# Memory keys and values as three rounded products instead of one fp32 product, and one tile's output products issued before a wait

## The chip, the cores and the metric

One core of a Trainium2 chip runs the whole kernel. The metric is device time in microseconds of one execution; the median of 3 runs of the kernel before is 2779.76 us (2779.39 to 2781.21).

## The reference, cut to what matters

Two transformer-like blocks follow each other on 1024 tokens of width 1024, all in fp32. The change lies in the first: after its mixing and attention the sum goes through an output projection, and a cross-attention to 256 memory tokens comes next.

```python
x = x + jnp.concatenate([y_f, y_a], axis=-1) @ w_out[l]
x = x + memory_cross_attention(rms_norm(x, g_mem_q[l]), rms_norm(mem, g_mem_kv[l]),
                               w_mem_q[l], w_mem_kv[l], w_mem_o[l])
...
def memory_cross_attention(hq, mn, w_mem_q, w_mem_kv, w_mem_o):
    q = (hq @ w_mem_q).reshape(B, S, MEM_HEADS, MEM_HEAD_DIM)
    k, v = jnp.split(mn @ w_mem_kv, 2, axis=-1)      # mn: 256 x 1024, w_mem_kv: 1024 x 2048
    s = jnp.einsum("bshd,bmhd->bhsm", q, k).astype(jnp.float32) * (MEM_HEAD_DIM ** -0.5)
    p = jax.nn.softmax(s, axis=-1).astype(v.dtype)
    o = jnp.einsum("bhsm,bmhd->bshd", p, v).reshape(B, S, D)
    return o @ w_mem_o
```

A mixture of experts and the second block follow; the change does not touch them.

## The kernel before, in words

The program is written out engine by engine, each engine's instructions in a fixed order with semaphores between them. PSUM has eight banks; a helper (`Bank`, line 87 on) gives each product a bank in turn, `begin` makes TensorE wait until the bank's last use is read, `end` signals that it is full, `wait` lets a reader wait for that, `done` and `read` tell and await that it has been read out.

Most products are made in three passes: an operand is rounded to fp32r (`hi`), the rest is kept as a second fp32r part (`lo`), and the product is hi*hi + hi*lo + lo*hi, each an fp32r matmul. ScalarE makes `hi` with a copy, VectorE (or GpSimd) makes `lo` with a subtraction, often in the place of the raw data. The memory keys and values are an exception: they are plain fp32 products. The stages around the change, in order:

- **End of the first attention.** Heads' outputs are gathered in four chunks of 128 features (`mixa`). Chunks 0 to 2 are rounded and split early; chunk 3 comes from the very last heads: ScalarE copies (line 1440), VectorE adds and multiplies (2075, 2076), ScalarE rounds the chunk (1404) and VectorE makes its remainder (2078, signal `block1_lo`).
- **Output products `y1`** (loop at 2797). For each of 8 token tiles and both halves j of the columns, `mixed(t, j, k)` (2750) gives three matmuls of 512 columns for chunk k. Tile 0's products with chunks 0 to 2 are issued already inside the attention's loop, behind the transposes of the last two score tiles; the wait for `block1_lo` comes next, then chunk 3 of tile 0, then tiles 1 to 7 whole. VectorE adds each result to X (`mixed_in`, 2079; addition at 2084). Before tile 7 TensorE transposes the normalised memory tokens (`nm`), and VectorE multiplies the gain in (`gained`, 1889) into `mnT`.
- **Key loop** (2813). For c in 0 to 7: one block `mk`, eight fp32 products of a 128x128 weight tile with the 256 memory tokens (line 2820), then the two groups of transposes of token tile c (`n2`, line 2591), after a wait for the normalised tile. ScalarE's loop (1458): squares of tile c (1287), the rounded copies of the tokens of tile c-1 (1456), then the copy of key block c out of PSUM (1279). GpSimd makes the reciprocal root (1018, 1019). VectorE's loop: scaling of tile t (1885), then the two remainders of its tokens (2101).
- **Value loop** (2825). Eight blocks `mv` through the helper `product` (2605). ScalarE rounds each (1478), VectorE makes its remainder (2118). After blocks 0 to 3 ScalarE and VectorE split the first half of the query weights (`mem_round`, line 1473, and `mem_rest`, line 2111), after block 7 the second half.
- **Query products `mq`** (2831). Three passes, 512 columns, 24 matmuls a block.

Weights come over SyncE's queue into a ring of three 2 MB slots (`fetch`, issues at 909). The memory weights are four pieces `mkv0` to `mkv3`: `mkv0` is fetched at the attention's end, `mkv1` and `mkv2` are issued when the last `y1` product is done, `mkv3` after key block 3, the query weights `mq0` after key block 7 and `mq1` after value block 3.

Of the kernel before, what the change touches and what calls it, by code (L numbers as in the profile page):

```python
# [137 lines left out]
def build(nc, A, out):  # L138
    sems = {}
    ctx = ExitStack()  # L140
    with ctx:
# [490 lines left out]
        memx = mem(GB0, 2048).rearrange("p (m d) -> p m d", m=2)  # L632
        mnT = mem(SPARE, 2048).rearrange("p (k s) -> p k s", k=KC)
        KM = mem(GB0 + 4096, 2048).rearrange("p (k s) -> p k s", k=KC)
        VT_hi, VT_lo = (mem_r(at_, 2048).rearrange("p (c s) -> p c s", c=8) for at_ in (GB0 + 6144, HN_AT))
# [640 lines left out]
        def _(act):  # L1276
# [173 lines left out]
            for m in range(2):  # L1450
                act.wait_ge(sem(f"mem_in{m}"), 16)
                square(memx[:, m, :], D, st[:, 48 + m:49 + m], HN[m]).then_inc(sem("norm_ssq"), 1)
            def token_hi(t):
                for j in range(2):
                    b = bk.wait(act, ("n2", t, j))
                    nc.scalar.activation(xm_hi[t // 4][:, 4 * j:4 * j + 4, tile(t % 4)], b4(b), ACT.Copy).then_inc(sem("psum_hi"), 1)

            for c in range(8):
                bk.read(act, ("y1", c, 1))
                bk.wait(act, ("n2", c - 2, 1) if c >= 2 else ("nm", c, 1))  # L1460
                square(X[:, c, :], D, st[:, 52 + c:53 + c], HN[c % 2]).then_inc(sem("norm_ssq"), 1)
                if c >= 1:
                    token_hi(c - 1)
                b = bk.wait(act, ("mk", c))
                copy(("mk", c), KM[:, c, :], PS[:, b, 0:MEM])
# [8 lines left out]

            for n in range(2):
                for c in range(4 * n, 4 * n + 4):
                    b = bk.wait(act, ("mv", c))
                    nc.scalar.activation(VT_hi[:, c, :], PS[:, b, 0:MEM], ACT.Copy).then_inc(sem("psum_hi"), 1)
                mem_round(f"mq{n}", R_MQ)
            for c, h in MQ:  # L1480
# [387 lines left out]
        def _(dve):  # L1868
# [210 lines left out]
            def mixed_in(t):  # L2079
                dve.wait_ge(sem(f"x_tile{t}"), 64)  # L2080
                for j in range(2):
                    b = bk.wait(dve, ("y1", t, j))
                    x = X[:, t, NB * j:NB * j + NB]
                    bk.done(v.tensor_tensor(x, x, PS[:, b, :], ALU.add), ("y1", t, j))

            for t in range(T - 1):
                mixed_in(t)
                if t >= T - 3:
                    m = t - (T - 3)
                    scaled("nm", m, memx[:, m, :], HN[m], st[:, 50 + m:51 + m])  # L2090
            for j in range(2):
                for m in range(2):
                    gained(("nm", m, j), mnT[:, 4 * j:4 * j + 4, tile(m)], R_MKV, 4 * j)
            mixed_in(T - 1)
            for t in range(T):
                scaled("n2", t, X[:, t, :], HN[t % 2], st[:, 60 + t:61 + t])
                for j in range(2):
                    dve.wait_ge(sem("psum_hi"), XM_HI + 2 * t + j + 1)
                    b = bk.at[("n2", t, j)][0]
                    hi, lo = (x[t // 4][:, 4 * j:4 * j + 4, tile(t % 4)] for x in (xm_hi, xm_lo))  # L2100
                    bk.done(v.tensor_tensor(lo, b4(b), value(hi), ALU.subtract), ("n2", t, j))

            def mem_rest(name, n, row=None, ks=range(KC)):
                for k in ks:
                    c = slice(NB * k, NB * k + NB)
                    dve.wait_ge(sem("part_hi"), n + k + 1)
                    lo, raw, hi = mem_lo[name][:, c], mem_raw[name][:, c], value(mem_hi[name][:, c])
# [5 lines left out]

            for n in range(2):
                for c in range(4 * n, 4 * n + 4):
                    dve.wait_ge(sem("psum_hi"), VT_HI + c + 1)
                    b = bk.at[("mv", c)][0]
                    bk.done(v.tensor_tensor(VT_lo[:, c, :], PS[:, b, 0:MEM], value(VT_hi[:, c, :]), ALU.subtract), ("mv", c))
                mem_rest(f"mq{n}", UP_N + KC * n, R_MQ)
            mem_rest("mo0", UP_N + 2 * KC)  # L2120
            for kind, t in att2_steps():
# [10 lines left out]
                elif kind == "vw":  # L2132
                    for h in range(4):
# [5 lines left out]
                        if t == 0 and h >= 2:  # L2139
                            mem_rest("mo1", UP_N + 3 * KC, None, range(4 * (h - 2), 4 * (h - 2) + 4))  # L2140
                elif kind == "pt":
# [445 lines left out]
        def _(pe):  # L2587
# [209 lines left out]
            for t in range(T):  # L2797
                if t == T - 1:
                    for m in range(2):
                        pe.wait_ge(sem("norm_hn"), HNORM["nm"] + m + 1)  # L2800
                        for j in range(2):
                            turns(("nm", m, j), HN[m][:, NB * j:NB * j + NB])
                for j in range(2):
                    if t >= 1:
                        bk.begin(pe, ("y1", t, j))
                        for k in range(3):
                            mixed(t, j, k)
                if t == 0:
                    pe.wait_ge(sem("block1_lo"), 8)
                for j in range(2):  # L2810
                    bk.end(mixed(t, j, 3), ("y1", t, j))

            for c in range(8):
                if c % 4 == 0:
                    w_wait(pe, f"mkv{c // 4}")
                b = bk.begin(pe, ("mk", c))
                for k in range(KC):
                    if c == 0 and k % 4 == 0:
                        bk.read(pe, ("nm", 0, k // 4)), bk.read(pe, ("nm", 1, k // 4))
                    ins = mm(PS[:, b, 0:MEM], wview(f"mkv{c // 4}")[:, k, tile(c % 4)], mnT[:, k, :], start=(k == 0), stop=(k == KC - 1))  # L2820
                bk.end(ins, ("mk", c))
                pe.wait_ge(sem("norm_hn"), HNORM["n2"] + c + 1)
                for j in range(2):
                    turns(("n2", c, j), HN[c % 2][:, NB * j:NB * j + NB])
            for c in range(8):
                if c % 4 == 0:
                    w_wait(pe, f"mkv{2 + c // 4}")
                product(("mv", c), lambda k: wview(f"mkv{2 + c // 4}")[:, k, tile(c % 4)], lambda k: mnT[:, k, :], KC, lambda b: PS[:, b, 0:MEM])
            for t in range(T):
                bk.read(pe, ("n2", t, 0)), bk.read(pe, ("n2", t, 1))  # L2830
            for c, h in MQ:
                w1, w2 = (x[f"mq{c // 4}"].rearrange("p (k n) -> p k n", k=KC) for x in (mem_hi, mem_lo))
                b = bk.begin(pe, ("mq", c, h))
                for k in range(KC):
                    if c % 4 == 0 and h == 0:
                        pe.wait_ge(sem("part_lo"), UP_N + KC * (c // 4) + k + 1)
                    x1, x2 = xm_hi[h][:, k, :], xm_lo[h][:, k, :]
                    mm(PS[:, b, :], w1[:, k, tile(c % 4)], x1, start=(k == 0), stop=False)
                    mm(PS[:, b, :], w1[:, k, tile(c % 4)], x2, start=False, stop=False)
                    ins = mm(PS[:, b, :], w2[:, k, tile(c % 4)], x1, start=False, stop=(k == KC - 1))  # L2840
                bk.end(ins, ("mq", c, h))
            for c in range(8):
                bk.read(pe, ("mk", c)), bk.read(pe, ("mq", c, 0))
            for kind, t in att2_steps():
# [11 lines left out]
                elif kind == "vw":  # L2856
# [4 lines left out]
                    for h in range(4):  # L2861
                        for d in range(2):
                            pe.wait_ge(sem("part_lo"), UP_N + KC * (2 + t) + 2 * h + d + 1)
                        for m in range(2):
# [349 lines left out]
```

## Time and profile before

| what | value |
|---|---|
| median of 3 runs | 2779.76 us |
| profiled execution | 2780.26 us |
| its span | 2778.3 us |
| TensorE matmul busy | 2726.2 us (98%) |
| weight loads busy | 2281.4 us (82%) |
| VectorE, ScalarE, GpSimd busy | 1800.1, 1259.2, 439.2 us |
| mean granted TensorE clock | 0.996 of 2.4 GHz |

Every row gives a start in microseconds from the start of the span and a duration. A matmul's record lasts longer than the distance to the next, since matmuls are pipelined: the distance of starts is the pace. Records of weight loads are shown as an operation of their own (PEld). Operands are named by the region of memory (`w_f` is the fp32 view of the ring, `w_f32r` its fp32r view, `ps` is PSUM). The bracket at the end of a row is the idle time of the engine before it and what ended it. The granted clock is a share of 2.4 GHz; 0.50 is 1.2 GHz.

### The profile page before, as it was taken

The page shows a single profiled execution, that of the slowest core. Times are in us where ns is not written, and L with a number is a line of the kernel's source. Part 1 is how long each engine was busy: PE and PEld are TensorE (multiplying, and loading weights), DVE is VectorE, ACT ScalarE, POOL GpSimd, SP SyncE. Part 2 cuts the span into 40 slices and gives each one's busy share as a digit, 9 for nine tenths or more (in the row PEclk, how much of TensorE's full clock was granted, in tenths as well). Part 3 has the DMA queues.
Part 4 walks back from the last instruction along what each step waited for, and adds up shares of the span by engine and source line. Part 5 has one row for each costly group of instructions (what it writes and reads, how often), then busy time and mean ns, then how long its engine had stood idle before and what let it go on. Part 6 is the DMA issues. An engine that isn't in the chain of part 4 may idle for free.

```text
span 2778.3 us, 36356 instructions
## 1 busy us (share of the span) xinstructions
PE 2726.2 (98%) x14436; PEld 2281.4 (82%) x14436; DVE 1800.1 (65%) x2497; ACT 1259.2 (45%) x2026; POOL 439.2 (16%) x393
## 2 busy tenths in 40 slices
PE   8999999999999999999999999999999999999998
PEld 7978888788884888888888887878888868888898
DVE  3646888330546888888885968988886572110575
ACT  4333787141432777777776124454454453111101
POOL 1500231000011211111102000000001043221341
PEclk9999999999999999999999999999999999999999
DMA  4041000420217999999982121030121221110141
GB/s 140 31 154 46 31 1 1 165 93 32 92 67 294 391 396 396 396 396 396 395 326 69 61 104 49 20 118 28 60 72 42 94 76 46 46 46 31 60 145 61
DMA packets 141604, 379.79 MB, mean 137 GB/s; under 512 B 11952, under 2 KB 45234, under 8 KB 141309
## 3 DMA queue, kind: packets, MB, share of 16 engines
q1 hardware_dynamic: 126140, 325.22, 30.9%
q0 software_dynamic: 12560, 42.74, 4.9%
q10 hardware_dynamic: 2736, 9.50, 0.9%
q8 instruction: 116, 1.90, 0.3%
q14 instruction: 52, 0.42, 0.0%
HBM read 341.13 MB, written 35.26 MB: 135 GB/s over the span
## 4 chain that ended last, share of the span: by engine, by line
PE 91%; DVE 4%; ACT 2%; DMA 1%; issue 1%; POOL 0%; SPq 0%; ACTq 0%; POOLq 0%; DVEq 0%
PE ps L2988 8%; PE ps L2989 8%; PE ps L2990 8%; PE ps L2591 7%; PE ps L2973 6%; PE ps L2975 6%; PE ps L2974 6%; PE ps L3082 3%; PE ps L3084 3%; PE ps L3083 3%; PE ps L2605 3%; PE ps L3129 2%; PE ps L3094 1%; PE ps L3096 1%; PE ps L3095 1%; PE ps L3114 1%
## 5 line engine op out<-in xcount | busy, mean ns | idle before, releaser
L2310 DVE SCALAR_TENSOR_TENSOR b_f<-b_f,small_f 128x1023 f32<-128x1023 f32 (+14 forms) x240 | 304.3, 1268 | 27.0 <-ACT small_f L1279 13.8
L2988 PE MATMUL ps<-x_f32r,w_f32r 128*128 128x512 f32 x480 | 187.9, 392 | 4.3 <-DVE b_f L2507 3.6
L2990 PE MATMUL ps<-x_f32r,w_f32r 128*128 128x512 f32 x480 | 187.4, 390 | 0.0
L2974 PE MATMUL ps<-w_f32r,a_f32r 128*128 128x512 f32 x456 | 177.4, 389 | 0.0
L2989 PE MATMUL ps<-ht_f32r,w_f32r 128*128 128x512 f32 x416 | 162.5, 391 | 0.0
L3083 PE MATMUL ps<-w_f32r,a_f32r 128*128 128x512 f32 x384 | 149.9, 390 | 0.0
L2974 PE MATMUL ps<-x_f32r,a_f32r 128*128 128x512 f32 x312 | 121.4, 389 | 0.0
L1279 ACT ACTIVATE x_f<-ps 128x512 f32<-128x512 f32 (+1 forms) x184 | 91.0, 533 | 44.4 <-PE ps L2591 21.0
L1209 POOL TENSOR_TENSOR w_f32r<-w_f,w_f32r 128x2048 fp32r<-128x2048 f32 x23 | 110.2, 4793 | 1.9
L2988 PEld LDWEIGHTS ps<-x_f32r,w_f32r 128*128 128x128 f32 x480 | 90.4, 188 | 23.7 <-issue 4.9
L2990 PEld LDWEIGHTS ps<-x_f32r,w_f32r 128*128 128x128 f32 x480 | 90.5, 189 | 18.9
L2200 DVE TENSOR_TENSOR w_f32r<-w_f,c_f32r 128x2048 fp32r<-128x2048 f32 x38 | 86.1, 2285 | 26.3 <-ACT c_f32r L1540 26.3
L2973 PE MATMUL ps<-c_f32r,a_f32r 128*128 128x512 f32 x256 | 101.0, 394 | 0.3 <-issue 0.3
L2973 PE MATMUL ps<-ht_f32r,a_f32r 128*128 128x512 f32 x256 | 101.2, 395 | 0.0
L2973 PE MATMUL ps<-b_f32r,a_f32r 128*128 128x512 f32 x256 | 99.7, 389 | 0.3 <-issue 0.3
L2975 PE MATMUL ps<-ht_f32r,a_f32r 128*128 128x512 f32 x256 | 99.9, 390 | 0.0
L2974 PEld LDWEIGHTS ps<-w_f32r,a_f32r 128*128 128x128 f32 x456 | 85.7, 188 | 17.2
L2975 PE MATMUL ps<-b_f32r,a_f32r 128*128 128x512 f32 x256 | 99.7, 389 | 0.0
L2975 PE MATMUL ps<-c_f32r,a_f32r 128*128 128x512 f32 x256 | 99.7, 389 | 0.0
L2988 PE MATMUL ps<-ht_f32r,w_f32r 128*128 128x512 f32 x256 | 99.6, 389 | 0.0
L2990 PE MATMUL ps<-ht_f32r,w_f32r 128*128 128x512 f32 x256 | 99.6, 389 | 0.0
L2057 DVE TENSOR_REDUCE small_f<-ps 128x1 f32<-128x1024 f32 x64 | 78.1, 1220 | 30.8 <-PE ps L2770 30.3
(578 smaller groups left out, 7870.6 us busy)
## 6 DMA issues: line engine op xcount, KB each, us to landing
w_f<-in_w_exp_up SPq DMA_DIRECT2D x40, 1024.0 KB, 10.3
w_f<-in_w_exp_down SPq DMA_DIRECT2D x38, 1024.0 KB, 10.2
w_f<-in_w_exp_gate SPq DMA_DIRECT2D x36, 1024.0 KB, 8.8
x_f<-in_w_exp_gate SPq DMA_DIRECT2D x28, 1024.0 KB, 8.6
x_f<-in_w_exp_down SPq DMA_DIRECT2D x26, 1024.0 KB, 11.0
x_f<-in_w_exp_up SPq DMA_DIRECT2D x24, 1024.0 KB, 10.3
w_f<-in_w_in SPq DMA_DIRECT2D x22, 1024.0 KB, 5.1
w_f<-in_w_in SPq DMA_DIRECT2D x10, 2048.0 KB, 8.1
```

The lines of the kernel that those rows point to most:

```text
L1209: nc.gpsimd.tensor_tensor(mem_r(slot, k * n), mem(slot, k * n), value(mem_r(slot + 2048, k * n)), ALU.subtract).then_inc(sem("split"), 1)
L1279: ins = nc.scalar.activation(dst, src, ACT.Copy, scale=scale)
L2200: v.tensor_tensor(unit_lo(n), unit_raw(n), value(unit_hi(n)), ALU.subtract).then_inc(sem("unit_lo"), 1)
L2310: ins = v.scalar_tensor_tensor(C_conv[k][:, d:S], U_conv[k][:, 0:S - d], cols[:, k, R_TAP + j:R_TAP + j + 1], C_conv[k][:, d:S], ALU.mult, ...
L2591: return nc.tensor.transpose(dst, src, ident[0:n, 0:n])
L2973: mm(o, x1, w1[:, k, c], start=(kk == 0), stop=False)
L2974: mm(o, x1, w2[:, k, c], start=False, stop=False)
L2975: ins = mm(o, x2, w1[:, k, c], start=False, stop=(kk == KC - 1))
L2988: mm(o, l1, r1, start=(k == 0), stop=False)
L2989: mm(o, l1, r2, start=False, stop=False)
L2990: ins = mm(o, l2, r1, start=False, stop=(k == n - 1))
L3083: mm(PS[:, b, :], x1[:, k, :], lo[:, k, :], start=False, stop=False)
```

## The change

`y1`: TensorE issues tile 1's products with chunks 0 to 2 right before the wait for chunk 3, and tile 1 later adds only its chunk 3.

Keys and values: each of the 16 blocks becomes 24 fp32r matmuls of 256 columns (`mem_columns`). For block p ScalarE rounds a column chunk of 128 of its 2 MB weight piece (8 x 128 elements on each partition) into one of six buffers (`mkv_round`), and VectorE puts the remainder in the place of the raw weights (`mkv_rest`). The memory tokens are split too, in two halves. ScalarE and VectorE run two blocks ahead of TensorE; blocks 2 to 5 wait for the last `y1` product, since their buffers lie where the output weights were. The rounding of the first query weight piece moves: chunks 4 to 7 after value block 5, chunks 0 to 3 (their home holds the rounded tokens) after block 7, and TensorE takes the chunks in that order.

```diff
+        mn_lo, mn_hi = (mem_r(at_, 2048).rearrange("p (k s) -> p k s", k=KC) for at_ in (SPARE, GC0))
+        MKV_N = 18
+        MQ_ORDER = {"mq0": [4, 5, 6, 7, 0, 1, 2, 3]}
+        mkv_home = [GC0 + 2048, GC0 + 3072] + [GA0 + 1024 * i for i in range(4)]
+        def mkv_parts(p):
+            at_, c = W0 + 4096 * wslot(seq[f"mkv{p // 4}"]), tile(p % 4)
+            raw, lo = (x.rearrange("p (k n) -> p k n", k=KC)[:, :, c] for x in (mem(at_, 4096), mem_r(at_, 4096)))
+            return raw, mem_r(mkv_home[p % 6], 1024).rearrange("p (k n) -> p k n", k=KC), lo
...
+            def mkv_round(p):
+                w_wait(act, f"mkv{p // 4}")
+                if 2 <= p < 6:
+                    bk.wait(act, ("y1", T - 1, 1))
+                elif p >= 6:
+                    bk.wait(act, ("mk", p - 6) if p < 14 else ("mv", p - 14))
+                raw, hi, lo = mkv_parts(p)
+                nc.scalar.activation(hi, raw, ACT.Copy).then_inc(sem("part_hi"), 1)
+            mkv_round(0)
+            mkv_round(1)
+            for j in range(2):
+                bk.read(act, ("nm", 0, j)), bk.read(act, ("nm", 1, j))
+                nc.scalar.activation(mn_hi[:, 4 * j:4 * j + 4, :], mnT[:, 4 * j:4 * j + 4, :], ACT.Copy).then_inc(sem("part_hi"), 1)
...
                 if c >= 1:
                     token_hi(c - 1)
+                mkv_round(c + 2)
                 b = bk.wait(act, ("mk", c))
...
-            for n in range(2):
-                for c in range(4 * n, 4 * n + 4):
-                    b = bk.wait(act, ("mv", c))
-                    nc.scalar.activation(VT_hi[:, c, :], PS[:, b, 0:MEM], ACT.Copy).then_inc(sem("psum_hi"), 1)
-                mem_round(f"mq{n}", R_MQ)
+            for c in range(8):
+                if c < 6:
+                    mkv_round(c + 10)
+                b = bk.wait(act, ("mv", c))
+                nc.scalar.activation(VT_hi[:, c, :], PS[:, b, 0:MEM], ACT.Copy).then_inc(sem("psum_hi"), 1)
+                if c == 5:
+                    mem_round("mq0", R_MQ, range(4, 8))
+            mem_round("mq0", R_MQ, range(0, 4))
+            mem_round("mq1", R_MQ)
...
+            def mkv_rest(p):
+                dve.wait_ge(sem("part_hi"), UP_N + (p + 1 if p < 2 else p + 3))
+                raw, hi, lo = mkv_parts(p)
+                v.tensor_tensor(lo, raw, value(hi), ALU.subtract).then_inc(sem("part_lo"), 1)
             for t in range(T - 1):
                 mixed_in(t)
+                if 3 <= t < 5:
+                    mkv_rest(t - 3)
...
+            for j in range(2):
+                dve.wait_ge(sem("part_hi"), UP_N + 3 + j)
+                c = slice(4 * j, 4 * j + 4)
+                v.tensor_tensor(mn_lo[:, c, :], mnT[:, c, :], value(mn_hi[:, c, :]), ALU.subtract).then_inc(sem("part_lo"), 1)
             mixed_in(T - 1)
             for t in range(T):
                 scaled("n2", t, X[:, t, :], HN[t % 2], st[:, 60 + t:61 + t])
+                mkv_rest(t + 2)
...
+            for c in range(8):
+                if c < 6:
+                    mkv_rest(c + 10)
+                dve.wait_ge(sem("psum_hi"), VT_HI + c + 1)
+                b = bk.at[("mv", c)][0]
+                bk.done(v.tensor_tensor(VT_lo[:, c, :], PS[:, b, 0:MEM], value(VT_hi[:, c, :]), ALU.subtract), ("mv", c))
+                if c == 5:
+                    mem_rest("mq0", UP_N + MKV_N, R_MQ, range(4, 8))
+            mem_rest("mq0", UP_N + MKV_N, R_MQ, range(0, 4))
+            mem_rest("mq1", UP_N + MKV_N + KC, R_MQ)
...
-                for j in range(2):
-                    if t >= 1:
-                        bk.begin(pe, ("y1", t, j))
+                for u in ([1] if t == 0 else [t] if t >= 2 else []):
+                    for j in range(2):
+                        bk.begin(pe, ("y1", u, j))
                         for k in range(3):
-                            mixed(t, j, k)
+                            mixed(u, j, k)
                 if t == 0:
                     pe.wait_ge(sem("block1_lo"), 8)
...
+            def mem_columns(name, p):
+                raw, w1, w2 = mkv_parts(p)
+                b = bk.begin(pe, name)
+                o = PS[:, b, 0:MEM]
+                if p >= 2:
+                    pe.wait_ge(sem("part_lo"), UP_N + p + 3)
+                for k in range(KC):
+                    if p == 0 and k % 4 == 0:
+                        pe.wait_ge(sem("part_lo"), UP_N + 3 + k // 4)
+                    mm(o, w1[:, k, :], mn_hi[:, k, :], start=(k == 0), stop=False)
+                    mm(o, w1[:, k, :], mn_lo[:, k, :], start=False, stop=False)
+                    ins = mm(o, w2[:, k, :], mn_hi[:, k, :], start=False, stop=(k == KC - 1))
+                bk.end(ins, name)
...
```

## Rows read from the trace of the kernel before

**Rows 1.** The page: the head, then the engines of the chain that ended last.

```profile
span 2778.3 us, 36356 instructions
...
PE 91%; DVE 4%; ACT 2%; DMA 1%; issue 1%; POOL 0%; SPq 0%; ACTq 0%; POOLq 0%; DVEq 0%
```

**Rows 2.** Groups by line, each shape apart, 484 to 700 us: busy us, mean ns.

```profile
L2820 PE MATMUL ps<-spare_f,w_f 128*128 128x256 f32 x128 | 28.9, 379 | 0.0
L2605 PE MATMUL ps<-spare_f,w_f 128*128 128x256 f32 x128 | 27.8, 379 | 0.0
```

**Rows 3.** TensorE in order of time, 480 to 612 us: start, duration, line, idle before.

```profile
494.54 0.38 PE L2591 MATMUL ps<-small_f 128*128 128x128 f32 x2
498.72 0.79 PE L2753 MATMUL ps<-a_f32r,w_f32r 128*128 128x512 f32 x1 [3.80 <-DVE w_f32r L2078]
...
504.00 0.41 PE L2753 MATMUL ps<-a_f32r,w_f32r 128*128 128x512 f32 x1
...
505.16 0.39 PE L2755 MATMUL ps<-ht_f32r,w_f32r 128*128 128x512 f32 x1
...
511.96 0.39 PE L2755 MATMUL ps<-a_f32r,w_f32r 128*128 128x512 f32 x1
```

**Rows 4.** Stretches: length, busy per engine (TensorE, weight loads, VectorE, ScalarE, GpSimd), clock.

```profile
500.00:504.00 4.00, 4.00 (x10) 3.04 (x10) 1.28 (x2) 0.89 (x1) 0.00 (x0) 0.50 1.02 407
504.00:508.00 4.00, 4.00 (x19) 3.32 (x18) 0.30 (x1) 1.41 (x4) 0.77 (x2) 1.00 1.03 414
```

**Rows 5.** The chain that ended last, 470 to 720 us, in order of time.

```profile
497.44 1.24 DVE w_f32r L2078
```

**Rows 6.** All engines in order of time, 532 to 580 us: one turn of the key loop.

```profile
543.34 3.61 PE L2820 MATMUL ps<-spare_f,w_f 128*128 128x256 f32 x16
...
559.78 1.04 PE L2591 MATMUL ps<-small_f 128*128 128x128 f32 x8
559.98 0.39 ACT L1279 ACTIVATE b_f<-ps 128x256 f32<-128x256 f32 x1 [1.93 <-PE ps L2820]
560.26 1.05 ACT L1287 ACTIVATE small_f<-x_f 128x1024 f32<-128x1024 f32 x1
...
560.65 3.62 PE L2820 MATMUL ps<-spare_f,w_f 128*128 128x256 f32 x16
...
561.30 1.07 ACT L1456 ACTIVATE ht_f32r<-ps 128x512 fp32r<-128x512 f32 x2
...
561.92 1.29 DVE L2101 TENSOR_TENSOR ht_f32r<-ps,ht_f32r 128x512 fp32r<-128x512 f32 x2 [2.38 <-ACT ht_f32r L1456]
563.12 0.74 DVE L1885 TENSOR_SCALAR small_f<-x_f,small_f 128x1024 f32<-128x1024 f32 x1
...
564.11 1.04 PE L2591 MATMUL ps<-small_f 128*128 128x128 f32 x8
```

**Rows 7.** Line 2989, each shape apart: duration ns min/median/max, first and last start.

```profile
L2989 PEld LDWEIGHTS ps<-w_f32r,a_f32r x256: 188/192/192, 2678.6 to 2770.4; 128*128 128x128 f32 x128
L2989 PE MATMUL ps<-w_f32r,a_f32r x256: 283/283/283, 2678.7 to 2770.5; 128*128 128x256 f32 x128
```

**Rows 8.** TensorE in order of time again, where transposes give way to fp32r matmuls.

```profile
485.40 0.47 PE L2753 MATMUL ps<-ht_f32r,w_f32r 128*128 128x512 f32 x1
485.71 0.39 PE L2754 MATMUL ps<-ht_f32r,w_f32r 128*128 128x512 f32 x1
```

**Rows 9.** Lines 1404 and 2078, each shape apart, 380 to 720 us.

```profile
L1404 ACT ACTIVATE w_f32r<-w_f x3: 1053/1056/1057, 392.5 to 496.3; 128x1024 fp32r<-128x1024 f32 x3
...
L2078 DVE TENSOR_TENSOR w_f32r<-w_f,w_f32r x1: 1226/1226/1226, 497.4 to 497.4; 128x1024 fp32r<-128x1024 f32 x1
```

**Rows 10.** DMA issues of 543.3 to 543.8 us: count, KB each, us to landing.

```profile
w_f<-in_w_mem_kv SPq DMA_DIRECT2D x1, 2048.0 KB, 7.8
```

**Rows 11.** Lines 1473 and 2111, each shape apart, 380 to 720 us.

```profile
L1473 ACT ACTIVATE c_f32r<-w_f,small_f x8: 707/708/712, 592.3 to 596.5; 128x512 fp32r<-128x512 f32 x8
...
L2111 DVE SCALAR_TENSOR_TENSOR w_f32r<-w_f,small_f,c_f32r x8: 744/746/753, 593.0 to 597.7; 128x512 fp32r<-128x512 f32 x8
```

More of the change, by code:

```diff
@@ L2105, in mem_rest @@
                     c = slice(NB * k, NB * k + NB)
-                    dve.wait_ge(sem("part_hi"), n + k + 1)
+                    dve.wait_ge(sem("part_hi"), n + MQ_ORDER.get(name, list(range(KC))).index(k) + 1)
                     lo, raw, hi = mem_lo[name][:, c], mem_raw[name][:, c], value(mem_hi[name][:, c])
@@ L2112, in mem_rest @@
                     ins.then_inc(sem("part_lo"), 1)
[L2114 to L2120, printed above, removed]
+            for c in range(8):
[8 more added lines that the diff above has]
+            mem_rest("mq1", UP_N + MKV_N + KC, R_MQ)
+            mem_rest("mo0", UP_N + MKV_N + 2 * KC)
             for kind, t in att2_steps():
@@ L2139, in _ @@
                         if t == 0 and h >= 2:
-                            mem_rest("mo1", UP_N + 3 * KC, None, range(4 * (h - 2), 4 * (h - 2) + 4))
+                            mem_rest("mo1", UP_N + MKV_N + 3 * KC, None, range(4 * (h - 2), 4 * (h - 2) + 4))
                 elif kind == "pt":
@@ L2811, in _ @@
                     bk.end(mixed(t, j, 3), ("y1", t, j))
-            for c in range(8):
[L2814 to L2821, printed above, removed]
+            def mem_columns(name, p):
[11 more added lines that the diff above has]
+                bk.end(ins, name)
+            for c in range(8):
+                mem_columns(("mk", c), c)
                 pe.wait_ge(sem("norm_hn"), HNORM["n2"] + c + 1)
@@ L2825, in _ @@
             for c in range(8):
-                if c % 4 == 0:
-                    w_wait(pe, f"mkv{2 + c // 4}")
-                product(("mv", c), lambda k: wview(f"mkv{2 + c // 4}")[:, k, tile(c % 4)], lambda k: mnT[:, k, :], KC, lambda b: PS[:, b, 0:MEM])
+                mem_columns(("mv", c), 8 + c)
             for t in range(T):
@@ L2833, in _ @@
                 b = bk.begin(pe, ("mq", c, h))
-                for k in range(KC):
+                order = MQ_ORDER.get(f"mq{c // 4}", list(range(KC)))
+                for i, k in enumerate(order):
                     if c % 4 == 0 and h == 0:
-                        pe.wait_ge(sem("part_lo"), UP_N + KC * (c // 4) + k + 1)
+                        pe.wait_ge(sem("part_lo"), UP_N + MKV_N + KC * (c // 4) + i + 1)
                     x1, x2 = xm_hi[h][:, k, :], xm_lo[h][:, k, :]
-                    mm(PS[:, b, :], w1[:, k, tile(c % 4)], x1, start=(k == 0), stop=False)
+                    mm(PS[:, b, :], w1[:, k, tile(c % 4)], x1, start=(i == 0), stop=False)
                     mm(PS[:, b, :], w1[:, k, tile(c % 4)], x2, start=False, stop=False)
-                    ins = mm(PS[:, b, :], w2[:, k, tile(c % 4)], x1, start=False, stop=(k == KC - 1))
+                    ins = mm(PS[:, b, :], w2[:, k, tile(c % 4)], x1, start=False, stop=(i == KC - 1))
                 bk.end(ins, ("mq", c, h))
@@ L2862, in _ @@
                         for d in range(2):
-                            pe.wait_ge(sem("part_lo"), UP_N + KC * (2 + t) + 2 * h + d + 1)
+                            pe.wait_ge(sem("part_lo"), UP_N + MKV_N + KC * (2 + t) + 2 * h + d + 1)
                         for m in range(2):
```

## The prediction

> **What bounds the kernel now.** I read the page first: TensorE is on the chain that ended last for 91% of a span of 2778.3 us [rows 1], so a change pays when it shortens TensorE's own stream or closes a hole in it. The profiled execution took 2780.26 us, 2.0 more than its span and 0.5 more than the median of the runs (2779.76). Sums are differences within the profiled execution, taken off the median at the end.
>
> Next the groups by line, for the two sets of memory products. Each fp32 product is two matmul records, so 128 records are 64 products, and the two groups together keep TensorE busy without a hole [rows 2]. One block of 16 records runs from 560.65 to 564.11: 3.46 us, or 216 ns for a record [rows 6]. Sixteen blocks are 55.4 us.
>
> Then TensorE in order of time, where the first attention ends. It issues its last transposes at 494.54 (0.38 us), and the next matmul starts at 498.72 with 3.80 us of idle before it, released by VectorE's remainder of the last mixed chunk [rows 3, 5]. The twelve matmuls from 498.72 to 504.00 take 5.28 us; thirty at 505.16 to 511.96 take 6.80, so 0.227 each. The granted clock says why: 0.50 from 500 to 504, which is the 1.2 GHz level, and 1.00 right after, the 2.4 GHz level [rows 4]. Before it fell TensorE had stood idle for those 3.80 us.
>
> Last, one turn of the key loop, engine by engine [rows 6]. TensorE never stands there, but this hides a chain nearly as long as its own work, which matters below.
>
> **Part 1, the second tile's products ahead of the wait.** Six groups of three matmuls (two column halves, three chunks) move from behind the wait to ahead of it; they need chunks 0 to 2 alone, and banks 2 and 3, which the last score tile left before its transposes. Nothing is added, no DMA is moved. 18 x 0.227 = 4.1 us of work goes into a hole of 3.80 us, and the hole is gone: 3.8 us won. TensorE then never stops, so the clock should not fall: 5.28 - 12 x 0.227 = 2.6 us more. Two tiles now end close together; VectorE's two additions per tile, of the size of the remainders in [rows 6] (1.29 us), fit easily in the 24 x 0.227 = 5.4 us that TensorE spends on a tile, so that costs nothing. Part 1: **6.4 us**.
>
> **Part 2, three rounded passes.** 128 fp32 products of 432 ns become 384 fp32r matmuls of 256 columns. The trace has that form with three passes: line 2989 and its two neighbours run 256 each from 2678.7 to 2770.5, 91.8 us over 765 gaps, 0.120 us each with a weight load per matmul [rows 7]. A block becomes 24 x 0.120 = 2.88 us, all sixteen 46.1: **9.3 us** won. I take 0.120 as it is the same mix; the bounds are 0.108 (the half of an fp32 record's 216 ns) and 0.192, a load in the open, which is a rival below.
>
> Against it stands a small loss: after transposes the first fp32r matmul keeps 0.31 us to the next instead of 0.23 [rows 8]. Eight switches in the key loop: 0.6 us.
>
> **Part 2's new work.** ScalarE gets a rounding copy of 1024 elements per block, 1.06 us as line 1404, VectorE a subtraction of 1.23 us as line 2078 [rows 9]: sixteen of each, and two of each for the memory tokens. What covers each:
> - *Blocks 0 and 1 and the tokens.* The two blocks fall between the additions, in that same idle. The tokens' parts must be there when the key products start: VectorE has four gain multiplications of about 0.65 and two subtractions of 1.23 to do, 5.1 us, while TensorE has its last transposes and the last tile, 0.87 + 5.4 = 6.3; ScalarE's two copies run beside them. Nothing; without the 1.2 us to spare, at most the second subtraction's 1.2 us.
> - *Key loop, ScalarE.* From the key copy to the end of the token copies it now takes 559.98 to 562.37, 2.4 us [rows 6]; with 1.06 more it is 3.5, against a TensorE turn of 2.88 + 0.08 + 0.87 = 3.83. It fits by 0.4 us. The copy stands before the wait for the next key block, behind everything that the token chain needs of this turn.
> - *Key loop, VectorE.* 1.29 + 0.74 + 1.23 = 3.3 us a turn, also under 3.83, and the subtraction stands behind the scaling that TensorE waits for.
> - *Weights.* ScalarE now needs the second 2 MB piece for block 4 in its third turn, not TensorE in the fifth. It is issued as the y products end and lands 7.8 us later [rows 10]; ScalarE asks for it 2.88 + 3.83 + 2.5 = 9.2 us after the key products start. About 1.2 us to spare. If it were late, the delay would pass into copies and the chain, and cost its own length.
> - *Value loop.* A turn is 2.88 us; ScalarE has 1.06 and a copy of 256 columns (0.39 in [rows 6]), VectorE 1.23 and under 0.65: covered. The six buffers for rounded parts are handed back six blocks earlier.
> - *Query weights.* The low half of their rounded home holds the tokens' rounded part until the last value block. So four pieces come after it, and TensorE begins with the other four: 12 x 0.227 = 2.7 us of cover. The first late piece needs a copy of 0.39, then 0.71 and 0.75 [rows 11], ready at 1.9; VectorE's pace of 0.75 a piece against TensorE's 0.68 eats 0.2 more. Nothing, with 0.6 us to spare; without it the price is about 2 us once.
>
> **What is late next: the token chain.** The end of issue of a key block (559.78) releases the key copy (559.98), the squares (560.26), the two token copies (561.30), VectorE's two remainders (561.92), the next scaling (563.12 to 563.86), and only then the next token's transposes, at 564.11: 4.33 us from block to transposes [rows 6]. TensorE's own turn before is 0.87 + 3.46 = 4.33, so the chain is hidden with nothing to spare. After the change the own turn is 3.83. A wait s at one set of transposes also moves the next block back, so the next wait is 0.50 - s: waits alternate between 0.5 and 0, four in seven turns, **2.0 us** lost. Bounds: 0 (part of the 4.33 was the queue and not the chain) and 8 x 0.5 = 4.0 us (each turn at 4.33).
>
> **Sum.** 6.4 + 9.3 - 0.6 - 2.0 = 13.1 us. Everything behind waits for TensorE's progress (the query products follow at once, the later weights are fetched when blocks end), so the gain is kept to the end: 2779.76 - 13.1 = **2766.7 us**; for the profiled execution 2767.2.
>
> **Rivals.**
> - *TensorE's work alone sets the key loop.* For it: no idle shows today. Against: the scaling ends 0.25 us before the transposes, too close to be free. Gain 15.1: 2764.7 us.
> - *ScalarE or the chain holds every turn at 4.33.* If the strided rounding copy takes over 0.4 us more than line 1404's, ScalarE is the bound. The key loop then wins nothing, the value loop 8 x 0.58: gain 6.4 + 4.6 = 11.0, 2768.8 us. A late second weight piece lands near here too.
> - *The clock falls all the same.* It fell after idle; with no idle nothing in these rows lets it fall. 2.6 us less: 2769.3 us.
> - *The moved products do not start early.* If a bank or operand is held, part 1 is worth nothing: gain 6.7, 2773.1 us, still 0.24% down. Against: chunk 2's parts are used the same way for tile 0 before the hole.
> - *Slower: weight loads in the open.* The place is the sixteen blocks, which have three loads where fp32 had two records. A load lasts 0.192 us [rows 7]. If matmuls of 256 columns could not hide it, 384 x 0.192 = 73.7 us, 18.3 over today, less 6.4: 2791.7 us. It decides from 0.161 us per matmul ((55.4 + 6.4) / 384). Against: 0.120 measured, loads included, over 768 matmuls with weights from the same kind of memory.
>
> The Trainium skill speaks for this last rival: the page TensorE: Matmul & The Clock Gate gives a load of 128 columns as columns over 1.2, so 107 ns (section LDWEIGHTS), and keeps the faster load from fp32 (section Weight-path perf modes). As an estimate from that page, load and 256 columns in series are 0.213 us and the kernel would take about 2800 us; the same page also says that loads are pulled ahead of running matmuls (section Step-by-step: what each phase is for). Lines 2988 to 2990, at 0.120, bear out the pulling ahead [rows 7].
>
> **How the numbers follow.** A measurement of this kernel can tell about 0.2% (5.6 us) from no change. Chances: forecast 0.54, TensorE alone 0.19, every turn at 4.33 or late weights 0.14, clock 0.04, moved products held 0.03, loads in the open 0.03, and 0.03 for something unseen that brings it within 0.2%. The range of 2763 to 2771 reaches from TensorE alone with a pace a little under 0.120 to the clock rival with a further 1.7 us of waits. All cases but the last two (loads, unseen) are over 0.2% faster; with some doubt kept for the held products: faster 0.92, within 0.2% 0.05, slower 0.03.
>
> **What would show it.** Right: no idle before the last chunk's products, clock 1.00 from 492 to 508, key products starting near 536.9 instead of 543.34; a block of 24 at 2.88 us; transposes of every second token waiting on VectorE's scaling for some 0.5 us; the query products starting some 13 us earlier and not waiting for a late piece. Wrong: a block over 3.2 us, ScalarE busy through the whole loop, a wait for the second weight piece, or a span that falls much less than the start of the query products moved, which would mean that the gain is given back later.

## The result and the profile after

The kernel after takes 2765.67 us (median of 5 runs, 2765.03 to 2767.89) against 2779.76 for the kernel before, also of 5: the medians differ by 14.1 us. The ratio is 0.9947 with a 95% interval of 0.9937 to 0.9958. 2766.7 was forecast, with 2763 to 2771 as the range. One execution of the kernel after in a later measurement (3384.06 us at a mean granted clock of 0.752) is left out of every figure here.

The profiled execution has a span of 2763.3 us. First the page of the kernel after, which answers to [rows 1]: the head, the engines' busy times and the chain.

```profile
span 2763.3 us, 36673 instructions
...
PE 2713.0 (98%) x14564; PEld 2275.6 (82%) x14564; DVE 1821.2 (66%) x2515; ACT 1276.2 (46%) x2044; POOL 441.0 (16%) x393
...
PE 91%; DVE 5%; ACT 2%; issue 1%; DMA 1%; POOL 0%; ACTq 0%; POOLq 0%; DVEq 0%
```

There are 128 TensorE instructions more (384 for 256) and 18 more each on VectorE and ScalarE, and the span is still 15.0 us shorter. TensorE's busy time falls by 13.2 us. VectorE's share of the chain rises from 4 to 5%. That fits the forecast of a new wait on it, but a rounded share of 2763 us cannot show a few microseconds; the rows below do.

Then TensorE in order of time around the old hole, which answers to [rows 3].

```profile
493.80 0.38 PE L2639 MATMUL ps<-small_f 128*128 128x128 f32 x2
493.94 0.48 PE L2801 MATMUL ps<-ht_f32r,w_f32r 128*128 128x512 f32 x1
...
498.15 0.39 PE L2801 MATMUL ps<-a_f32r,w_f32r 128*128 128x512 f32 x1
```

No idle stands in a bracket: the moved 18 matmuls fill 493.94 to 498.15, 0.234 us each, where the hole was. The granted clock of the same stretches, which answers to [rows 4]:

```profile
496.00:500.00 4.00, 4.00 (x20) 3.25 (x19) 1.23 (x1) 0.67 (x1) 0.00 (x0) 1.00 0.97 374
500.00:504.00 4.00, 4.00 (x19) 3.34 (x18) 1.55 (x3) 1.15 (x2) 0.59 (x2) 1.00 1.03 418
```

It is 1.00, the 2.4 GHz level, where it was 0.65 and 0.50 in the kernel before. The last transposes of the attention start at 493.80, 0.74 us sooner than before, although nothing ahead of them was edited. So I compare distances. **Stage A**, from those transposes to the first key matmul, was 543.34 - 494.54 = 48.80 us and is 536.12 - 493.80 = 42.32: 6.48 won. **Stage K**, from there to the first query matmul, was 605.41 - 543.34 = 62.07 and is 590.36 - 536.12 = 54.24: 7.83 won. In both traces the first query matmul has a successor: 0.42 us later before (605.83), 0.23 after (590.59), which is another 0.19. These give 14.5 of the 15.0 us. The 0.74 ahead of the stages more than covers the rest: behind those two starts the spans agree to 0.24 us (2172.47 and 2172.71), so the gain is kept to the end.

The key loop, from TensorE, ScalarE and VectorE in order of time (three views of the kernel after, one fence for each); it answers to [rows 6].

```profile
536.12 0.28 PE L2870 MATMUL ps<-c_f32r 128*128 128x256 f32 x1
...
538.95 1.03 PE L2639 MATMUL ps<-small_f 128*128 128x128 f32 x8
539.74 0.36 PE L2870 MATMUL ps<-c_f32r 128*128 128x256 f32 x1
...
543.10 1.09 PE L2639 MATMUL ps<-small_f 128*128 128x128 f32 x8 [0.29 <-DVE small_f L1917]
543.95 0.36 PE L2870 MATMUL ps<-c_f32r,a_f32r 128*128 128x256 f32 x1
...
546.86 1.03 PE L2639 MATMUL ps<-small_f 128*128 128x128 f32 x8
...
551.00 1.09 PE L2639 MATMUL ps<-small_f 128*128 128x128 f32 x8 [0.29 <-DVE small_f L1917]
```

```profile
542.85 0.38 ACT L1290 ACTIVATE b_f<-ps 128x256 f32<-128x256 f32 x1 [0.35 <-PE ps L2872]
543.12 1.05 ACT L1298 ACTIVATE small_f<-x_f 128x1024 f32<-128x1024 f32 x1
...
544.16 1.08 ACT L1483 ACTIVATE ht_f32r<-ps 128x512 fp32r<-128x512 f32 x2
545.12 1.07 ACT L1472 ACTIVATE a_f32r<-w_f 128x1024 fp32r<-128x1024 f32 x1
```

```profile
541.09 1.29 DVE L2145 TENSOR_TENSOR ht_f32r<-ps,ht_f32r 128x512 fp32r<-128x512 f32 x2 [2.28 <-ACT ht_f32r L1483]
542.30 0.74 DVE L1917 TENSOR_SCALAR small_f<-x_f,small_f 128x1024 f32<-128x1024 f32 x1
542.96 1.22 DVE L2121 TENSOR_TENSOR w_f32r<-w_f,a_f32r 128x1024 fp32r<-128x1024 f32 x1
```

A block is 538.95 - 536.12 = 2.83 us, 24 x 0.118. Every second set of transposes waits on the scaling (line 1917): 543.10, 551.00, then 558.91 and 566.82. The block that starts at 539.74 + 0.08 = 539.82 (its own start and the short first gap) is issued by 542.65, and the transposes start at 543.10: a wait of 0.45 us. The bracket counts 0.29, since the records of pipelined matmuls reach into the wait. The pair of turns shows a little more: 551.00 - 543.10 = 7.90 us, where TensorE's own work is 2 x (0.87 + 2.83) = 7.40. Beside the 0.45, the first matmul behind transposes that waited stands 0.85 us after them (543.95) and not 0.79 (539.74 behind 538.95). So a wait costs 0.5 us, and four of them 2.0. Line 1472's rounding copy fits in ScalarE's turn, with 0.35 us of idle after it in the tight turns (the bracket at 542.85).

### The profile page after: what moved, and what is told of

The parts are those of the page before. It is cut to its first block, busy times and chain, and to the rows that moved or that the text cites. A ratio compares the mean times of both kernels' runs of the same rounds, so it can differ in the third digit from the quotient of the medians.

```text
span 2763.3 us, 36673 instructions
## 1 busy us (share of the span) xinstructions
PE 2713.0 (98%) x14564; PEld 2275.6 (82%) x14564; DVE 1821.2 (66%) x2515; ACT 1276.2 (46%) x2044; POOL 441.0 (16%) x393
## 4 chain that ended last, share of the span: by engine, by line
PE 91%; DVE 5%; ACT 2%; issue 1%; DMA 1%; POOL 0%; ACTq 0%; POOLq 0%; DVEq 0%
PE ps L3042 8%; PE ps L3044 8%; PE ps L3043 8%; PE ps L2639 6%; PE ps L3027 6%; PE ps L3029 6%; PE ps L3028 6%; PE ps L3136 3%; PE ps L3138 3%; PE ps L3137 3%; PE ps L3183 2%; PE ps L2653 2%; PE ps L3148 1%; PE ps L3150 1%; PE ps L3149 1%; PE ps L3168 1%
```

## The experiments

Every run is compared with the kernel before on its own chip; stages A and K are taken from its profile as above. The medians of the kernel before were 2780.47 us beside the first four, 2780.75 beside the next four, 2780.38 beside the last.

### Part 1 alone

```diff
-                for j in range(2):
-                    if t >= 1:
-                        bk.begin(pe, ("y1", t, j))
+                for u in ([1] if t == 0 else [t] if t >= 2 else []):
+                    for j in range(2):
+                        bk.begin(pe, ("y1", u, j))
```

> The kernel before with part 1 alone (tile 1's products with chunks 0 to 2 ahead of the wait). Theory: 3.8 us of hole and 2.6 us of lost clock come back, 6.4 us, about 2773.3 us; the key products start near 536.9 instead of 543.34, the granted clock is 1.00 through 496 to 504. Rival, the clock falls for another reason than the idle time: 3.8 us, 2776.0, clock below 1.00 after 496. Rival, the products do not start early: 2779.8.

2774.32 us, 6.2 less; ratio 0.9981 (0.9972 to 0.9990). Stage A is 536.26 - 493.94 = 42.32, as in the kernel after to the hundredth; stage K is 62.08, as before. The clock is 1.00 from 488 to 508. The forecast's 6.4 us stands as 6.48.

### Part 2 alone

The kernel after with the edit above undone.

> The kernel after with part 1 undone (three rounded passes alone). Theory: key products to query products take 54.2 to 54.5 us as in the kernel after against 62.1 to 62.5 before, 8.0 us won, about 2771.8 us, with four waits of some 0.44 us on VectorE's scaling in the key loop, and the hole of 3.8 us and the clock of 0.50 back. Rival, the two parts share something (the hole's length or the clock also helps the key loop): the gains of this run and of part 1 alone do not add up to the 14.1 us of the whole.

2772.09 us, 8.4 less; ratio 0.9971 (0.9960 to 0.9982). Stage A is 48.72, stage K 54.24. The hole and the slow clock are back, as TensorE in order of time and the clock of that run show:

```profile
498.37 0.79 PE L2801 MATMUL ps<-a_f32r,w_f32r 128*128 128x512 f32 x1 [3.80 <-DVE w_f32r L2110]
```

```profile
496.00:500.00 4.00, 1.64 (x4) 1.35 (x5) 1.23 (x1) 1.05 (x1) 0.07 (x1) 0.58 1.00 381
500.00:504.00 4.00, 4.00 (x12) 3.14 (x11) 1.28 (x2) 1.15 (x2) 0.05 (x1) 0.56 1.02 406
```

The two parts add up (6.2 + 8.4 = 14.6 by the medians, 14.1 measured together), and neither stage shows anything of the other part. The rival of a shared gain falls.

### The hole filled with nothing useful

```diff
                 if t == 0:
+                    bk.begin(pe, ("y1", 1, 0))
+                    for i in range(16):
+                        mm(PS[:, bk.at[("y1", 1, 0)][0], :], mixa_hi[:, 0, tile(1)], wo_hi[0][:, 0:NB], start=True, stop=True)
                     pe.wait_ge(sem("block1_lo"), 8)
```

> The kernel before, with 16 throwaway matmuls of 512 columns (3.6 us) in the hole ahead of the last chunk's wait, into a bank whose next product overwrites them. Nothing useful is moved, so only the clock can win. Theory: the idle time is what lowers the clock; it stays at 1.00, the twelve matmuls that took 5.28 us take 2.7, and the gain is 2.6 us, 2777.2. Rival, the clock falls whatever TensorE does here: 0, and 2779.8.

2778.78 us, 1.7 less; ratio 0.9991 (0.9982 to 1.0). The median alone would not settle it; the trace does. TensorE in order of time, then the clock, of this run:

```profile
494.42 3.92 PE L2811 MATMUL ps<-ht_f32r,w_f32r 128*128 128x512 f32 x16
498.46 0.50 PE L2753 MATMUL ps<-a_f32r,w_f32r 128*128 128x512 f32 x1
```

```profile
500.00:504.00 4.00, 4.00 (x19) 3.32 (x18) 1.29 (x2) 0.96 (x1) 0.00 (x0) 1.00 1.03 422
```

Stage A is 540.65 - 494.28 = 46.37, so 2.4 us shorter with no work moved, against 2.6 forecast for the clock. The last chunk's products start 4.18 us after the last transposes, exactly as in the kernel before (498.46 - 494.28 and 498.72 - 494.54), so none of this is the hole. Idle time is what lowered the clock here, and part 1's 6.48 us are two things of their own: 2.43 of clock and the other 4.05 of hole.

### The scaling ahead of the remainders

```diff
+            scaled("n2", 0, X[:, 0, :], HN[0], st[:, 60:61])
             for t in range(T):
-                scaled("n2", t, X[:, t, :], HN[t % 2], st[:, 60 + t:61 + t])
                 mkv_rest(t + 2)
+                if t + 1 < T:
+                    scaled("n2", t + 1, X[:, t + 1, :], HN[(t + 1) % 2], st[:, 61 + t:62 + t])
                 for j in range(2):
```

> The kernel after, with VectorE's scaling of the next token tile ahead of the two remainders of this one. Theory, the chain from key block over token copies and remainders to the scaling makes TensorE wait in every second turn: the chain gets 1.3 us shorter, the four waits of 0.44 us go, 1.8 us won over the kernel after, about 2763.9. Rival, the wait comes from the squares or from the reciprocal root on GpSimd, which stand ahead of the scaling in both orders: waits stay, 2765.7. Rival, the remainders become late and TensorE or ScalarE waits for those: 2765.7 or more.

2764.84 us; ratio 0.9943 (0.9930 to 0.9957). The time is within the scatter of the kernel after, so the stages must tell. Stage A is 42.35, stage K 592.58 - 540.04 = 52.54: 1.70 us won over the kernel after, 1.8 forecast. No bracket of TensorE names the scaling in the key loop (TensorE in order of time):

```profile
542.87 1.03 PE L2641 MATMUL ps<-small_f 128*128 128x128 f32 x8
546.57 1.03 PE L2641 MATMUL ps<-small_f 128*128 128x128 f32 x8
...
557.66 1.06 PE L2641 MATMUL ps<-small_f 128*128 128x128 f32 x8
561.44 1.09 PE L2641 MATMUL ps<-small_f 128*128 128x128 f32 x8
565.24 1.09 PE L2641 MATMUL ps<-small_f 128*128 128x128 f32 x8
569.04 1.09 PE L2641 MATMUL ps<-small_f 128*128 128x128 f32 x8
```

The first turns are 3.70, which is 0.87 + 2.83. The chain over the remainders was the cause. But the last three turns are 3.78, 3.80 and 3.80, so a second chain is near. GpSimd, then VectorE in order of time, same run:

```profile
544.57 0.19 POOL L1029 TENSOR_SCALAR small_f<-small_f 128x1 f32<-128x1 f32 x1 [5.24 <-ACT small_f L1298]
...
548.27 0.29 POOL L1029 TENSOR_SCALAR small_f<-small_f 128x1 f32<-128x1 f32 x1 [2.88 <-ACT small_f L1298]
...
555.67 0.49 POOL L1029 TENSOR_SCALAR small_f<-small_f 128x1 f32<-128x1 f32 x1 [2.68 <-ACT small_f L1298]
...
563.10 0.66 POOL L1029 TENSOR_SCALAR small_f<-small_f 128x1 f32<-128x1 f32 x1 [2.51 <-ACT small_f L1298]
```

```profile
547.30 1.22 DVE L2121 TENSOR_TENSOR w_f32r<-w_f,a_f32r 128x1024 fp32r<-128x1024 f32 x1
...
551.10 1.22 DVE L2121 TENSOR_TENSOR w_f32r<-w_f,a_f32r 128x1024 fp32r<-128x1024 f32 x1
```

An operation on one column grows from 0.19 to 0.66 us. It ends at 548.56 and 556.16, and VectorE's weight subtraction, which runs from 547.30 and 554.89 for 1.22 us, ends at 548.52 and 556.11. These two engines now form a ring: subtraction, GpSimd's two operations, the next scaling, the remainders, the next subtraction. It takes 551.10 - 547.30 = 3.80 us, 0.10 more than TensorE's turn, so the small operation is held 0.10 us longer in each turn (0.19, 0.29, 0.39, 0.49, 0.59) until the ring is the bound. A run below takes this up.

### One more rounding copy per turn

```diff
                 raw, hi, lo = mkv_parts(p)
+                if 2 <= p < 10:
+                    nc.scalar.activation(mem_r(GB0 + 6144 + 1024 * (p % 2), 1024).rearrange("p (k n) -> p k n", k=KC), raw, ACT.Copy)
                 nc.scalar.activation(hi, raw, ACT.Copy).then_inc(sem("part_hi"), 1)
```

> The kernel after, with one more rounding copy of 1024 elements by ScalarE in each of the eight turns of the key loop, into memory that is not used there. Theory: ScalarE's turn is 3.35 us in the kernel after against TensorE's mean of 3.95; with 0.95 more it is 4.3 and becomes the bound, every turn 4.3 long, so the key loop is 8 x 0.35 = 2.8 us longer than in the kernel after, about 2768.5 us; ScalarE shows no idle in the loop. Rival, the chain over VectorE stays the bound and ScalarE has room: nothing changes, 2765.7.

2769.37 us; ratio 0.9962 (0.9949 to 0.9975). Stage K is 594.90 - 539.30 = 55.60, 1.36 over the kernel after. ScalarE in order of time:

```profile
546.50 0.39 ACT L1290 ACTIVATE b_f<-ps 128x256 f32<-128x256 f32 x1
...
547.80 1.10 ACT L1485 ACTIVATE ht_f32r<-ps 128x512 fp32r<-128x512 f32 x2
548.76 1.09 ACT L1473 ACTIVATE b_f32r<-w_f 128x1024 fp32r<-128x1024 f32 x1
549.71 1.08 ACT L1474 ACTIVATE a_f32r<-w_f 128x1024 fp32r<-128x1024 f32 x1
550.65 0.41 ACT L1290 ACTIVATE b_f<-ps 128x256 f32<-128x256 f32 x1
```

ScalarE has no idle, its turn is 550.65 - 546.50 = 4.15, and all sets of transposes are about 4.17 apart. So ScalarE is the next bound, as said. The size was off: 4.15 and not 4.3, and in the kernel after its turn is 4.15 - 0.95 = 3.20 by starts and not 3.35. From the first to the last transposes of the loop it is 571.35 - 542.13 = 29.22 us, against 566.82 - 538.95 = 27.87 in the kernel after, seven turns each: that difference, 1.35, is the whole 1.36. One copy more than the change has costs 0.2 us a turn.

### The query pieces in their old order

The first query weight piece is rounded and split whole after value block 7 and used in the order 0 to 7 (`MQ_ORDER = {}`, one `mem_round` and one `mem_rest` behind the loop).

> The kernel after, with the first query weight piece rounded whole after the last value block and taken by TensorE in the order 0 to 7. Theory: the first piece is ready 0.39 + 0.71 + 0.75 = 1.9 us after the last value block, and VectorE's 0.75 a piece against TensorE's 0.68 adds 0.5 over the eight: TensorE stands for about 2.4 us, 2768.1 us. Rival, the clock also falls after this wait, as after the hole of 3.8 us: up to 2.6 us more, 2770.7. Rival, something else already delays the query products, so no change: 2765.7.

2770.05 us; ratio 0.9960 (0.9946 to 0.9975). Stage K is 56.37, 2.1 us more than the kernel after; 2.4 were expected. TensorE in order of time, then the stretch with its clock:

```profile
594.69 0.47 PE L2888 MATMUL ps<-ht_f32r,c_f32r 128*128 128x512 f32 x1 [1.96 <-DVE w_f32r L2153]
```

```profile
590.00:600.00 10.00, 8.04 (x47) 6.94 (x46) 7.06 (x12) 7.56 (x14) 0.00 (x0) 1.00 0.01 2
```

So the split order of the query pieces is worth 2.1 us: it is the cover that the forecast relied on. A wait of 1.96 us left the clock at 1.00, so the rival of a second fall does not hold here. The median is 3.3 us over that of the kernel after beside it (2766.74, below), 1.2 more than the stages show and within the scatter of whole times.

### Both waits taken away

Besides the hole stage A has one wait of TensorE, in the kernel before (at 536.92) and in the kernel after alike: the second memory token's transposes wait for VectorE's scaling of it. TensorE in order of time, kernel after:

```profile
528.10 1.03 PE L2639 MATMUL ps<-small_f 128*128 128x128 f32 x8
529.71 1.09 PE L2639 MATMUL ps<-small_f 128*128 128x128 f32 x8 [0.57 <-DVE small_f L1917]
```

This run has the scaling ahead of the remainders as above, and the memory tokens' scaling one tile earlier:

```diff
-                if t >= T - 3:
-                    m = t - (T - 3)
+                if T - 4 <= t < T - 2:
+                    m = t - (T - 4)
```

> The kernel after with the scaling ahead of the remainders (as in the run with the scaling first) and with the memory tokens scaled one tile earlier each, so that TensorE's transposes of them don't wait 0.57 us. Theory: four waits of 0.44 and one of 0.57 go, 2.3 us under the kernel after, about 2763.4 us; from the last transposes of the attention to the first query product 94.2 us instead of 96.5. Rival, the second scaling was late for another reason than its place in VectorE's order: 0.57 us stay, 2763.9.

2764.80 us (2764.18 to 2765.43); ratio 0.9943 (0.9930 to 0.9956). Stage A is 535.35 - 493.83 = 41.52, 0.80 shorter, where the bracket had 0.57. The two sets above are 1.61 us apart and eight transposes take 0.87, so by starts the wait was 0.74: the bracket counts too little here too. Stage K is 52.54. From the transposes to the first query matmul it is 94.06 us; the kernel after has 96.56. No bracket names the scaling any more, but the last three turns of the key loop are 3.77, 3.80 and 3.80, as with the scaling first.

### The kernel after once more

> The kernel after once more, beside the three before it. 2765.7 us within 1.5. Waits of 0.44 us at every second set of transposes again, and no idle or low clock from 490 to 510 us, while the stretches near 10 to 30, 840 to 910, 2250 and 2760 us may have the clock low or not in any execution; theory: these give the scatter between executions of one kernel.

2766.74 us (2765.93 to 2770.26, five executions) beside the three runs above; ratio 0.9952 (0.9939 to 0.9965). That is 1.1 over its first median, within the 1.5 us expected. The profiled execution is the slowest of the five, 2770.26 us. Its stages are the same to a few hundredths: A 538.87 - 496.57 = 42.30, K 54.21. What differs lies ahead of them: the last transposes start at 496.57 and not at 493.80. Stretches of the kernel after, first its first profile, then this one:

```profile
16.00:26.00 10.00, 7.04 (x56) 6.51 (x57) 9.46 (x17) 9.18 (x18) 2.33 (x7) 1.00 1.06 381
26.00:36.00 10.00, 10.00 (x50) 8.09 (x50) 2.71 (x5) 4.23 (x9) 0.00 (x0) 1.00 0.35 71
```

```profile
16.00:26.00 10.00, 5.93 (x51) 5.58 (x52) 9.42 (x17) 10.00 (x21) 2.97 (x8) 1.00 1.06 382
26.00:36.00 10.00, 10.00 (x38) 8.09 (x38) 3.75 (x6) 3.76 (x8) 0.00 (x0) 0.83 0.34 67
```

At the program's start, where the first weights are awaited, TensorE was less busy (5.93 of 10 us for 7.04) and the clock then lower (0.83). The other traces go the same way. From 26 to 36 us, where TensorE is busy all the time, the clock is 0.88, 0.93 and 0.90 with the scaling first, with one more copy and with the query pieces in their old order, and their last transposes start at 497.69, 496.96 and 495.96. In the seven traces where it is 1.00 there, they start at 493.80 to 494.54, also in the three whose clock is 0.83 in the ten microseconds before, in which TensorE waits anyway. This is seen, not tried: no run kept TensorE busy there, and the low clock need not be the whole delay.

### VectorE's subtraction out of GpSimd's way

The edit is shown against the run with both waits taken away.

```diff
             scaled("n2", 0, X[:, 0, :], HN[0], st[:, 60:61])
+            mkv_rest(2)
             for t in range(T):
-                mkv_rest(t + 2)
                 if t + 1 < T:
                     scaled("n2", t + 1, X[:, t + 1, :], HN[(t + 1) % 2], st[:, 61 + t:62 + t])
+                    mkv_rest(t + 3)
```

> The run with both waits taken away, with VectorE's weight subtraction moved once more: it now follows the scaling of the next tile, so that it is over before GpSimd's reciprocal root of the tile after starts. In the run with the scaling first, GpSimd's first small operation grew from 0.19 to 0.66 us from turn to turn and ended each time as VectorE's subtraction ended, and the last turns were 3.78 to 3.80 us instead of 3.70. Theory, the two engines shut each other out of a path to SBUF: the operation takes 0.19 us in every turn again, all turns are 3.70, and the key products to the query products take 52.25 us instead of 52.54; in all 0.3 us less than there, about 2764.5 us, which the times can't tell, only the profile. Rival, the growth has another cause: it is there again, and 52.5 us stay.

2763.94 us (2763.74 to 2765.28); ratio 0.9943 (0.9929 to 0.9956). Stage K is 587.60 - 535.39 = 52.21, 52.25 forecast. GpSimd, then VectorE in order of time:

```profile
547.32 0.19 POOL L1029 TENSOR_SCALAR small_f<-small_f 128x1 f32<-128x1 f32 x1 [2.88 <-ACT small_f L1298]
547.59 0.55 POOL L1030 TENSOR_TENSOR small_f<-small_f 128x1 f32<-128x1 f32 x1
...
562.12 0.19 POOL L1029 TENSOR_SCALAR small_f<-small_f 128x1 f32<-128x1 f32 x1 [2.88 <-ACT small_f L1298]
```

```profile
546.63 1.28 DVE L2148 TENSOR_TENSOR ht_f32r<-ps,ht_f32r 128x512 fp32r<-128x512 f32 x2
```

It is 0.19 in every turn, and the turns are 3.70 (547.32 and 562.12 are four apart). VectorE is not idle beside it: it makes the remainders there, which read PSUM. So the growth came from the subtraction running beside it. This is the best version of the study: 16.4 us under the kernel before by the medians. In the two stages it is 42.32 + 54.24 - 41.52 - 52.21 = 2.83 us under the kernel after; the intervals of the whole times overlap, so that is shown by the traces alone.

## Why the prediction was right

- **The hole.** 3.8 + 2.6 = 6.4 us forecast, 6.48 by stage A, 6.2 by the run with part 1 alone. The filled hole shows the clock's share by itself, 2.4; the hole's is then 4.05. Each is off by about 0.2, in opposite directions. The 3.80 of the bracket was too short: the two last transposes take 493.94 - 493.80 = 0.14, and from 494.54 + 0.14 to 498.72 it is 4.04.
- **The blocks.** 0.120 us per matmul forecast from [rows 7], 0.118 measured: 384 x 0.002 = 0.8 us more won. The reading of the row was right: in the kernel before all 768 matmuls of lines 2988 to 2990 in that stretch are 0.11 to 0.13 apart, 0.120 in the mean, with no longer gap among them. Why the new blocks run 2 ns faster stays open. Against this, the sixteen old blocks were taken at 3.46 us each; the eight of the value loop took 605.41 - 577.97 = 27.44, so 3.43 each, 0.2 us less to win. The slower rival needed 0.161 and falls.
- **The switch from transposes.** This term was wrong. I charged 0.08 us eight times because the first fp32r matmul stands 0.31 from the next. In the kernel after the transposes last 539.74 - 538.95 = 0.79 and the first matmul behind them takes 0.08 more than the others (0.20 to its successor at 539.94, not 0.12), 0.87 together, and [rows 6] show 0.87 from transposes to fp32 matmuls too (559.78 to 560.65). It was in the turn already. 0.6 us were not lost.
- **A switch not forecast.** Where the fp32 value products gave way to the fp32r query products the first gap was 0.42; behind fp32r products it is 0.23. That is 0.19 us once.
- **The chain.** Waits in every second turn on VectorE's scaling: right in kind and place. The total was right too, but by luck. The transposes at 538.95 did not wait, so the next ones, at 543.10, come when the chain from the block before them lets them: 543.10 - 538.95 = 4.15 us is the chain with nothing else in it. The 4.33 of [rows 6] was TensorE's own turn, with the shorter chain inside it; the rows had it, since the scaling ends at 563.86, 4.08 us after the block, and 0.06 more pass from a scaling's end to the transposes that wait for it (542.30 + 0.74 = 543.04, and 543.10). The forecast had the chain 0.18 too long and TensorE's own turn 0.13 too long (3.83 for 3.70), and these nearly cancel: 0.45 for 0.50. The 0.06 behind each wait, not forecast, fills it up. The run with both waits gone and the subtraction moved has stage K at 52.21, so the waits cost 54.24 - 52.21 = 2.03 us where 2.0 were forecast; 1.70 of it came back with the scaling first, the rest when the ring over GpSimd was opened.
- **The covers.** ScalarE's turn fits by about 0.35 us as said. The query pieces' cover was worth 2.1 us. The second weight piece was tighter than said: it is issued at 536.32 and lands 8.4 us later, at 544.7 (the row of the DMA issues below), while its first copy starts at 545.12. 0.4 us were left, not 1.2.

```profile
w_f<-in_w_mem_kv SPq DMA_DIRECT2D x1, 2048.0 KB, 8.4
```

By terms 6.4 + 9.3 - 0.6 - 2.0 = 13.1 were forecast; in the stages it is 6.48 + 9.86 - 2.03 + 0.19 = 14.5, with 62.07 - 52.21 = 9.86 for the blocks and the switches where 9.3 - 0.6 = 8.7 were forecast. So the faster pace and the switch that cost nothing make up nearly all of the 1.4. The median's 14.1 lies between, within the runs' scatter.

## What to carry to other kernels

When the bounding engine is sped up, look for the chain that its own work has just covered; here it shows in every second turn once the work shrinks. A distance between two starts that equals the engine's own work says nothing of the chain's length: take that from the end of the chain's last link (here 4.08 us after the block, with starts 4.33 apart). A hole on TensorE can cost more than itself (here 4.05 us, and 2.43 more in clock), and work already at hand (here 18 matmuls with chunks that were ready) should be issued ahead of the wait. Compare distances between two marks around an edit rather than spans: here they repeat within 0.1 us where whole times scatter by 3 to 4.

## What the runs showed of the hardware that I had not expected

A GpSimd operation on 128x1 elements took 0.19 us alone and up to 0.66 us when it started during VectorE's 1.22 us subtraction with both inputs in SBUF; it ended 0.04 to 0.05 us after that subtraction. With the subtraction moved it was 0.19 again in all turns, although VectorE's remainders, with one input in PSUM, ran beside it (546.63 to 547.91 beside 547.32). In the kernel after it was 0.19 too; VectorE stood idle at those times. The Trainium skill's page SBUF — State Buffer, section SBUF: two separate sides, has VectorE and GpSimd share a pair of ports as an exclusive lock, taken also by a VectorE operation with two SBUF inputs against a GpSimd operation that reads SBUF; these runs agree, with the numbers above.

Where fp32 products gave way to fp32r products the first gap was 0.42 us in the kernel before and 0.41 with part 1 alone and with the filled hole, against 0.23 behind fp32r products. And executions of the same instructions differ by up to 3.9 us ahead of the edited stages (last transposes at 493.80 to 497.69 us over all traces, 493.80 and 496.57 for the kernel after), beside a granted clock that from 26 to 36 us is 1.00 in some and 0.83 to 0.93 in others; that the one makes the other was not tried.
